# Feed-forward products: the high weight part times both activation parts in one 512-column matmul, the two halves of the bank added on eviction

## What is computed

```
D_FF = 2816                          # 22 tiles of 128
def swiglu_ffn(x, w_gu, w_down):     # w_gu: 1024 x 5632, w_down: 2816 x 1024
    a, u = jnp.split(x @ w_gu, 2, axis=-1)
    return (jax.nn.silu(a) * u) @ w_down
...
x = layer_norm(DEEPNORM_ALPHA * x + 0.5 * swiglu_ffn(x, ffn1_w_gu[l], ffn1_w_down[l]), ln1_g[l], ln1_b[l])
```

## Time and profile before

| | before |
|---|---|
| median of 3 runs, us | 2691.51 |
| lowest and highest run, us | 2689.67, 2696.23 |
| the profiled execution's own time, us | 2694.33 |
| its span, first to last instruction, us | 2692.5 |
| TensorE matmul busy | 2320.4 us, 86% |
| TensorE weight load busy | 1644.3 us, 61% |
| VectorE busy | 937.8 us, 35% |
| ScalarE busy | 808.7 us, 30% |
| mean granted TensorE clock | 0.941 |

### The profile page before, as it was taken

One profiled execution on the slowest core, in us unless ns is written; L12 is line 12 of the kernel. 1 busy time (PEld: TensorE's weight loads), 2 busy tenths in 40 slices (PEclk: granted clock), 3 DMA queues, 4 the chain that ended last, 5 costly groups with the idle time before them and its releaser, 6 DMA issues.

```text
span 2692.5 us, 39307 instructions
## 1 busy us (share of the span) xinstructions
PE 2320.4 (86%) x14190; PEld 1644.3 (61%) x14191; DVE 937.8 (35%) x1589; ACT 808.7 (30%) x1317; POOL 165.9 (6%) x274
## 2 busy tenths in 40 slices
PE   5899858888888695888888789999899899998997
PEld 2445533333333592333333279988799899897997
DVE  0224030000000563000000065466655555566555
ACT  1222121111111331111111144345444444454444
POOL 0000001111111000111111100000000000000000
PEclk8899979999999797999999989999999999998999
DMA  9511759899999652999999684533355455424542
GB/s 395 222 62 63 270 209 428 371 428 427 428 417 382 241 188 91 426 428 428 418 419 422 264 285 158 170 141 126 131 168 168 162 179 152 141 95 157 188 144 76
DMA packets 301583, 677.57 MB, mean 252 GB/s; under 512 B 14808, under 2 KB 209368, under 8 KB 259472
## 3 DMA queue, kind: packets, MB, share of 16 engines
q1 hardware_dynamic: 289440, 659.05, 63.4%
q0 software_dynamic: 10720, 8.45, 1.0%
q10 hardware_dynamic: 1296, 8.32, 0.8%
HBM read 682.29 MB, written 20.19 MB: 261 GB/s over the span
## 4 chain that ended last, share of the span: by engine, by line
PE 77%; DMA 8%; DVE 7%; issue 4%; ACT 3%; SPq 1%; POOLq 0%; DVEq 0%; ACTq 0%; POOL 0%
PE ps L1629 28%; PE ps L1080 15%; PE ps L1100 8%; DMA ring<-in_moe_w_up 4%; PE ps L1842 3%; DMA ring<-in_w_mod 3%; PE ps L2007 2%; DVE arena L1293 1%; PE ps L690 1%; PE ps L1091 1%; PE ps L1081 1%; ACT arena L1157 1%; PE ps L1447 1%; PE ps L1448 1%; PE ps L1449 1%
## 5 line engine op out<-in xcount | busy, mean ns | idle before, releaser
L1629 PE MATMUL ps<-XS,WS 128*128 128x256 f32 x4224 | 518.4, 286 | 23.2 <-DVE XS L440 23.1
L1629 PEld LDWEIGHTS ps<-XS,WS 128*128 128x128 f32 x4224 | 515.6, 194 | 26.8 <-DVE XS L440 26.6
L1080 PE MATMUL ps<-ring,arena 128*64 128x512 f32 x1040 | 464.6, 600 | 63.1 <-issue 59.8
L1081 PE MATMUL ps<-ring,arena 128*64 128x512 f32 x1040 | 466.1, 601 | 0.0
L1614 DVE TENSOR_TENSOR WS<-ring,WS 128x1024 fp32r<-128x1024 f32 (+1 forms) x276 | 329.4, 1194 | 293.3 <-ACT WS L1609 293.0
L1609 ACT CAST WS<-ring 128x1024 fp32r<-128x1024 f32 (+1 forms) x276 | 281.9, 1022 | 431.4 <-PE ps L1629 415.1
L1080 PEld LDWEIGHTS ps<-ring,arena 128*64 128x64 f32 x1040 | 139.5, 138 | 352.4 <-issue 352.4
L1293 DVE TENSOR_TENSOR arena<-arena,ps 64x512 f32<-64x512 f32 x65 | 44.8, 690 | 855.1 <-ACT arena L1157 855.1
L1100 PE MATMUL ps<-ring,arena 128*64 128x512 f32 x520 | 272.0, 672 | 39.6 <-DVE arena L1296 39.6
L1101 PE MATMUL ps<-ring,arena 128*64 128x512 f32 x520 | 273.8, 676 | 0.0
L1629 PE MATMUL ps<-HS,WS 128*128 128x256 f32 x2112 | 262.2, 285 | 0.0
(11 more groups left out here) (273 smaller groups left out, 2570.9 us busy)
## 6 DMA issues: line engine op xcount, KB each, us to landing
ring<-in_moe_w_gate SPq DMA_DIRECT2D x64, 2048.0 KB, 16.5
ring<-in_moe_w_up SPq DMA_DIRECT2D x64, 2048.0 KB, 20.9
ring<-in_moe_w_down SPq DMA_DIRECT2D x64, 2048.0 KB, 19.4
ring<-in_ffn_w_gu SPq DMA_DIRECT2D x90, 1024.0 KB, 7.3
ring<-in_w_mod SPq DMA_DIRECT2D x24, 2048.0 KB, 16.7
ring<-in_ffn_w_down SPq DMA_DIRECT2D x32, 1408.0 KB, 6.4
ring<-in_w_in SPq DMA_DIRECT2D x10, 2048.0 KB, 7.8
ring<-in_conv_w_in SPq DMA_DIRECT2D x6, 2048.0 KB, 13.5
```

What stands on the lines that cost most here:

```text
L1080: pe.matmul(ps[0:CAP, 0, :], x, gate[:, j, c, :], start=k == 0, stop=k == KD - 1)
L1081: mm = pe.matmul(ps[CAP:P, 0, :], x, up[:, j, c, :], start=k == 0, stop=k == KD - 1)
L1629: mm = L.eng.matmul(out_ap, weights[:, i, :], moving[:, j, k, :], start=k == 0 and weights is wh and j == 0, stop=k == total - 1 and weigh ...
```

## The change

A network's `products` now streams the high and the low part of the activation through one load of the high weight, as one matmul of 512 columns into both halves of a bank, and then the high activation part through the low weight into the first half. ScalarE copies the second half out of the bank, VectorE adds the first half to it, and only then do silu, the product with the up tile, or the addition to the residual stream follow. The layout of banks and buffers is the same; SA and HF hold the copied halves.

```diff
@@ class Ffn, signals
+                self.low_kept = shared("ffn_low_kept", 2 * FFT, 2)
+                self.summed = shared("ffn_summed", FFT, 2)
...
+                self.y_low_kept = shared("ffn_y_low_kept", KD, 2)
@@ pe, products(u, bank, moving)
-                        for weights, j in ((wh, 0), (wh, 1), (wl, 0)):
-                            mm = L.eng.matmul(out_ap, weights[:, i, :], moving[:, j, k, :], start=k == 0 and weights is wh and j == 0,
-                                              stop=k == total - 1 and weights is wl)
+                        L.eng.matmul(ps[:, bank, :].rearrange("p (j t) -> p j t", j=2), wh[:, i, :], moving[:, :, k, :],
+                                     start=k == 0, stop=False)
+                        mm = L.eng.matmul(ps[:, bank, 0:TL], wl[:, i, :], moving[:, 0, k, :], start=False, stop=k == total - 1)
@@ act
+                def round_hidden(f):
+                    L.wait(self.hidden, f + 1)
+                    L.inc(act.copy(HS[:, 0, f, :], HF[f % 2]), self.h_high)
+
+                def keep_low(u, o, bank, signal):
+                    self.units_used(L, u + 1)
+                    L.inc(act.copy(o, ps[:, bank, TL:2 * TL]), signal)
+
                 for f in range(FFT):
                     round_weights(UNITS + 2 * f)
-                    self.units_used(L, 2 * f + 1)
                     if f >= 2:
                         L.wait(self.hidden, f - 1)
-                    L.inc(act.activation(SA[f % 2], ps[:, 2 * (f % 2), 0:TL], ACT.Silu), self.silu)
+                    keep_low(2 * f, SA[f % 2], 2 * (f % 2), self.low_kept)
+                    if f:
+                        round_hidden(f - 1)
                     round_weights(UNITS + 2 * f + 1)
-                    L.wait(self.hidden, f + 1)
-                    L.inc(act.copy(HS[:, 0, f, :], HF[f % 2]), self.h_high)
-                for u in range(UNITS + 2 * FFT, FFN_UNITS):
-                    round_weights(u)
+                    L.wait(self.summed, f + 1)
+                    L.inc(act.activation(SA[f % 2], SA[f % 2], ACT.Silu), self.silu)
+                    if f >= 2:
+                        L.wait(self.h_split, f - 1)
+                    keep_low(2 * f + 1, HF[f % 2], 2 * (f % 2) + 1, self.low_kept)
+                round_hidden(FFT - 1)
+                for m in range(KD):
+                    for third in range(3):
+                        round_weights(2 * FFT + UNITS + 3 * m + third)
+                    if m >= 2:
+                        L.wait(self.y_added, m - 1)
+                    keep_low(2 * FFT + 3 * m + 2, SA[m % 2], 4 + m % 2, self.y_low_kept)
 
                 stage, later = self.next
                 for u in range(UNITS):
@@ dve
+                def sum_parts(i, o, bank, signal=None):
+                    L.wait(self.low_kept, i + 1)
+                    L.inc(v.tensor_tensor(o, o, ps[:, bank, 0:TL], ALU.add), signal)
+
+                def split_hidden(f):
+                    L.wait(self.h_high, f + 1)
+                    L.inc(v.tensor_tensor(HS[:, 1, f, :], HF[f % 2], high(HS[:, 0, f, :]), ALU.subtract), self.h_split)
+
                 for f in range(FFT):
                     split_weights(UNITS + 2 * f)
+                    sum_parts(2 * f, SA[f % 2], 2 * (f % 2), self.summed)
+                    if f:
+                        split_hidden(f - 1)
+                    split_weights(UNITS + 2 * f + 1)
+                    sum_parts(2 * f + 1, HF[f % 2], 2 * (f % 2) + 1)
                     L.wait(self.silu, f + 1)
-                    self.units_used(L, 2 * f + 2)
-                    if f >= 2:
-                        L.wait(self.h_split, f - 1)
-                    L.inc(v.tensor_tensor(HF[f % 2], SA[f % 2], ps[:, 2 * (f % 2) + 1, 0:TL], ALU.mult), self.hidden)
-                    split_weights(UNITS + 2 * f + 1)
-                    L.wait(self.h_high, f + 1)
-                    L.inc(v.tensor_tensor(HS[:, 1, f, :], HF[f % 2], high(HS[:, 0, f, :]), ALU.subtract), self.h_split)
+                    L.join()
+                    L.inc(v.tensor_tensor(HF[f % 2], SA[f % 2], HF[f % 2], ALU.mult), self.hidden)
+                split_hidden(FFT - 1)
                 stage, later = self.next
                 for m in range(KD):
                     for third in range(3):
...
                     if m >= KD - 2:
                         stage.split_weights(L, m - (KD - 2), later)
-                    self.units_used(L, 2 * FFT + 3 * m + 3)
-                    L.inc(v.scalar_tensor_tensor(out=XT[:, m, 0:TL], in0=ps[:, 4 + m % 2, 0:TL], scalar=0.5 / ALPHA,
-                                                 in1=XT[:, m, 0:TL], op0=ALU.mult, op1=ALU.add), self.y_added)
+                    L.wait(self.y_low_kept, m + 1)
+                    y, xs = SA[m % 2], XT[:, m, 0:TL]
+                    L.inc(v.tensor_tensor(y, y, ps[:, 4 + m % 2, 0:TL], ALU.add))
+                    L.join()
+                    L.inc(v.scalar_tensor_tensor(out=xs, in0=y, scalar=0.5 / ALPHA, in1=xs, op0=ALU.mult, op1=ALU.add), self.y_added)
```

More of the change, by code:

```diff
@@ L146 @@
 ACT_PER_LAYER = 0
-DVE_PER_LAYER = 75
+DVE_PER_LAYER = 135
 SPLITS_PER_LAYER = 2 * FFN_UNITS + MIXER_UNITS
@@ L1616, in pe, with products @@
             def pe(self, L):
-                def products(u, out_ap, moving):
+                def products(u, bank, moving):
                     L.wait(self.w_split, u + 1)
@@ L1636, in pe @@
                     for a in range(2):
-                        products(2 * f + a, ps[:, 2 * (f % 2) + a, 0:TL], XS)
+                        products(2 * f + a, 2 * (f % 2) + a, XS)
                 for m in range(KD):
@@ L1641, in pe @@
                     for third in range(3):
-                        products(2 * FFT + 3 * m + third, ps[:, 4 + m % 2, 0:TL], HS)
+                        products(2 * FFT + 3 * m + third, 4 + m % 2, HS)
                     if m >= 1:
```

## The result

| | before | after |
|---|---|---|
| median of 22 runs, us | 2694.81 | 2698.57 |
| lowest and highest run, us | 2688.42, 2697.44 | 2691.72, 2706.01 |
| profiled execution's own time, us | 2694.33 | 2706.01 |
| its span, us | 2692.5 | 2704.2 |
| TensorE matmul busy | 2320.4 us | 2321.3 us |

The ratio after to before is 1.0018, with a 95% interval of 1.0011 to 1.0026: 3.8 us more by the medians, within the 0.3% that I had called no change. The forecast was +7.6 us. The profiled execution of after is the slowest of its 22, 7.4 us over their median, so the two profiles lie further apart (11.7 us) than the two kernels.

A forecast was written before the change was run, and what follows sets the result against it. TensorE's matmul-to-matmul distance was taken to bound the networks, and waiting their ends. Terms -18.8, +20.4 and +6 gave +7.6 us: 2701.9 from the profiled execution, 2699 from the median; range 2683 to 2713.

The forecast's parts named there:

- The products: Feed-forward matmuls: a tile falls from 359.5 to 350.6 ns, 8.9 ns less, gaining 18.8 us over 2112 tiles.
- The upper part of my own range: Products in the summed case: 8.9 to 13 ns gained a tile, 13 if each pair carries a fixed cost.
- The rule of the distance: TensorE matmul spacing: columns over 2.4 GHz plus 2.5 ns; by it the change would gain 5 us, not 19.
- Added copies and additions at nothing: 52 ScalarE copies and 52 VectorE additions a network, 21 and 22 us, fit in idle time and cost nothing.
- The wait among hidden tiles: Rival: hidden-tile chain of 6.1 us grows beyond 8.4; 0.1 us beyond is +9, 2708; chance 0.04.
- The end of a network: After the last product, ScalarE's and VectorE's order adds a 5.1 us chain per network, 20.4 us lost in four.
- The clock: TensorE idling brings half clock under line 569: 2 us a network, less 1.7 already there, 6 us lost.
- Sum: Whole kernel: -18.8 for products, +20.4 for ends, +6 for clock, making +7.6 us.
- The forecast's own signs: Wrong if a network's middle shortens by under 2 or over 6 us, or its end grows by under 4.
- the summed case: Whole kernel: the priced terms hold together, with an own range of 2690 to 2708 us; chance 0.66.
- The busy share of the loads: Weight loads busy 99% of a network; rival that they set the pace: net -30 us, 2662, chance 0.12.

The follow-up runs named there:

- The two later traces of the changed kernel: The changed kernel run again unaltered, twice: 2697.32 us beside a kernel with idle matmuls added, ratio to before 1.0019, and 2691.18 us in one run.
- The second experiment: The changed kernel with its 512-column matmul split into two 256-column ones, each with its own load, copies and additions kept: 2719.57 us, ratio 1.0092.

## Why the prediction held, point by point

- **The products.** Expected 8.9 ns a tile and 18.8 us, from line 1883. The first profile shows 18.7 us, but as a mean of two paces. A network at 346.7 and 349.2 gains 352 x 13.3 + 176 x 10.6 = 6.5 us by its tiles, one at 353.3 and 351 gains 352 x 6.7 + 176 x 8.8 = 3.9. Four make 26 or 16. The two later traces of the changed kernel, with all four networks at the good pace, have 24.3 and 24.5 us from first to last product. Alone, this part brought 24.9 us by the medians, and 21 when taken out of the changed kernel. So this term was sized too small by 2 to 6 us: the mean distance of line 1883 (230.8) was used beside a 256-column pair at 119.8, where the two together take 346.7 when the pace is good. The upper part of my own range, 13 ns for a fixed cost of a pair, is what the good pace and the pairs of 512 columns show.
- **The rule of the distance** (the Trainium skill, TensorE: Matmul & The Clock Gate, "Back-to-back issue gap"): 2.5 ns over the columns. The section gives this for an isolated matmul; for a stream of loads and matmuls, which is the case here, it gives about 131 ns for 512 columns, and the prediction left this out. Neither holds here: the excess is 13.3 and 13.4 ns, a pair of 512 takes 226.7, and the isolated rule's 5 us would have missed the 21 to 25 measured. The measurement decides.
- **Added copies and additions at nothing:** held. The second experiment has all of them and the 360.0 ns of the kernel before. The wait among hidden tiles did not appear: on the page of after, TensorE's idle time ahead of line 1631 is the 23.1 us in which it waits for line 440 at the networks' starts, and nothing from the hidden tiles:

```profile
L1631 PE MATMUL ps<-XS,WS 128*128 128x512 f32 x1408 | 504.1, 402 | 23.2 <-DVE XS L440 23.1
```
- **The end of a network:** 5.1 us expected, 4.9 to 5.1 measured in each, 20.0 in all where 20.4 was forecast, by the steps named.
- **The clock:** 6 us expected, which is 2 in each network less the 1.7 that the kernel before already has in one. Measured the same way, line 569 took 8.6, 5.2 and 5.0 us more than before in the three executions of the changed kernel. The place, the sign and the size were right. The 9.5 us that the idle matmuls gave back are to be held against the 8 before that subtraction.
- **Sum.** With -21 to -24.9, +20.0 and +5.0 to +8.6 the terms make 0 to 8 us; measured 3.8. The one term that was off is the products'. Part of why +7.6 came so near is luck: 18.8 us lies between the 16 and the 26 that the two paces give, and with the 24.4 of the two later traces in its place the forecast would have been +2.0. The 2699 us forecast for the changed kernel was met to 0.4 us, but it stood on a median of three runs, 2691.5, where 22 runs give 2694.8. Single executions scatter by more than the effect: the spans of the three that were profiled lie 11.7 us above, 3.2 below and 0.3 below that of the kernel before.
- **The forecast's own signs.** The ends grew by more than 4 us, line 569 took over 5 us in all four networks of the first profile, partly at half clock, and there is no idle time between hidden tiles. But the middle of a network was to shorten by 2 to 6 us. It shortened by 6.4, 4.0, 3.7 and 4.6 in the first trace, and by 5.5 to 6.6 in the two later ones, over 6 in two networks of each. By its own sign the price of the products was too low. Its range for the summed case, 2690 to 2708, starts too high as well: the bounds given with it add up to 2682 at the low end.
- **The busy share of the loads** did not say which of the two sets the pace: it went from 99 to 86% while a tile went from 360.0 to 346.7 or 353.3 ns. The prediction names Perfetto Trace Analysis in the Trainium skill ("Identifying the Most-Contended Engine") for it. That section asks for this share together with the share of the peak arithmetic rate that the matmuls reach, not for the one alone.

## What to carry to other kernels

Where two engines' work is written out in one order each, a new instruction that waits for the last result must not stand ahead of work that other engines need for something else: here the place of one copy and the subtractions cost 22.5 us, about all that the new matmul gained. Look at the end of each stage before the middle of it; reordering it turned a change worth nothing into one of 0.7%. And the time in which TensorE waited was paid twice here, once as a wait and once by the half clock under the matmuls that followed.

## What the runs showed of the hardware that I had not expected

- A stream of a 512-column and a 256-column pair locks into one of two paces, 346.7 or 353.3 ns for both, for a whole network of 190 us, and which one changes from network to network and from execution to execution of the same program. Three pairs of 256 had 360.0 in every network of every trace, a pair of 512 with one of 128 columns had 340.0 in all four, and two pairs of 512 had 453.3. From first to last product the two paces are 1.7 to 2.5 us apart in the same network of different traces, so up to 10 us an execution. The profiled executions of the changed kernel with 2706.0 and 2691.2 us are 14.8 apart: 5.6 in the products, 3.4 in line 569, and 5.3 in the start of the first network (1572.7 and 1567.4). What picks the pace is open; no run was made for it.
- A pair does not get shorter with its columns without end: with 128 columns to stream in place of 256, behind a load that stayed the same, a tile came down by 7 to 13 ns only.
- Matmuls that nobody reads, put into TensorE's idle time at the end of each network, made the way from there to the next network, or to the end of the program, 1.9 to 2.6 us shorter and not longer: 9.5 us in all by the medians.
